# Recurrent stage of a two-block model: 32 by 32 triangles inverted by substitution on VectorE, one matrix a partition, instead of by products on TensorE

## The reference, cut to what matters

```python
for d in range(2):                       # forward, then reversed in time
    r, k, v = mix(p_r, ...), mix(p_k, ...), mix(p_v, ...)
    decay = jnp.exp(-jnp.exp(w_log)); a = jax.nn.sigmoid(...)
    kk = kk / jnp.maximum(jnp.sqrt(jnp.sum(kk * kk)), 1e-12)
    y_sum += wkv7_scan(rh, decay, kh, vh, -kk, kk * ah, reverse=(d == 1))

def step(state, inp):                    # of wkv7_scan, one token
    sa = jnp.einsum('bhvk,bhk->bhv', state, a_t)
    state = state * w_t + sa[..., None] * b_t + v_t[..., None] * k_t
    return state, jnp.einsum('bhvk,bhk->bhv', state, r_t)
```

## Time and profile before

| | before |
|---|---|
| median of 3 runs | 2783.99 us (2780.99 to 2785.55) |
| the profiled execution, its own time | 2784.29 us |
| its span | 2782.4 us |
| PE busy in the span | 2543.8 us (91%) |
| DVE busy | 1214.9 us (44%) |
| ACT busy | 771.4 us (28%) |
| POOL busy | 61.2 us (2%) |
| stage `rwkv7`: first instruction to first of the next stage | 1346.6 to 1650.9 us |

### The profile page before, as it was taken

How to read it: one execution, slowest core, us unless ns; L and a number is a source line. 1 busy time by engine, 2 the same in 40 slices (tenths; PEclk the granted TensorE clock), 3 DMA queues, 4 the chain that set the end, 5 groups by cost and what they waited for, 6 DMA issues and landing times. The chain is left out here.

```text
span 2782.4 us, 48899 instructions
## 1 busy us (share of the span) xinstructions
PE 2543.8 (91%) x21256; PEld 1789.0 (64%) x21256; DVE 1214.9 (44%) x2020; ACT 771.4 (28%) x1266; POOL 61.2 (2%) x52
## 2 busy tenths in 40 slices
PE   8998888899999999899899989979898998889888
PEld 7997677799999998677677757643333333333222
DVE  7764766544466652566544458531111111111113
ACT  4221354442343431355233236321000000000001
POOL 1000022100000000000000000010000000000000
PEclk9999899999999999999999989999999999999999
DMA  5445441355322223333212112489999999999997
GB/s 161 141 130 119 95 169 58 123 190 166 118 92 92 92 93 124 137 117 125 90 55 97 51 73 90 172 335 432 429 431 431 430 430 432 429 431 431 430 431 295
DMA packets 143797, 609.68 MB, mean 219 GB/s; under 512 B 37536, under 2 KB 59168, under 8 KB 118560
## 3 DMA queue, kind: packets, MB, share of 16 engines
q1 hardware_dynamic: 114672, 571.68, 52.8%
q10 hardware_dynamic: 28912, 34.88, 3.9%
HBM read 566.68 MB, written 37.47 MB: 217 GB/s over the span
## 5 line engine op out<-in xcount | busy, mean ns | idle before, releaser
L3838 PE MATMUL moe_bank<-moe_ring,xg 128*64 128x512 f32 x2048 | 492.2, 624 | 86.5 <-DMA moe_ring<-in_w_exp_up 85.6
L3838 PEld LDWEIGHTS moe_bank<-moe_ring,xg 128*64 128x64 f32 x2048 | 155.0, 142 | 365.9 <-issue 357.2
L4128 DVE TENSOR_TENSOR moe_sg<-moe_sg,moe_bank 64x512 f32<-64x512 f32 x64 | 44.1, 689 | 576.5 <-ACT moe_sg L3996 576.5
L3868 PE MATMUL moe_bank<-moe_ring,moe_act_t 128*64 128x512 f32 x1008 | 227.0, 592 | 0.0
L68 PE MATMUL ffn_prod<-ffn_x_low,ffn_w_high 128*128 128x258 f32 x704 | 200.1, 284 | 5.8 <-PEq L138 5.8
L69 PE MATMUL ffn_prod<-ffn_x_high,ffn_w_low 128*128 128x258 f32 x704 | 200.0, 284 | 0.0
L68 PE MATMUL in_bank<-x_low,in_w_high 128*128 128x264 f32 x640 | 184.8, 289 | 16.4 <-DVE in_w_low L987 9.2
L70 PE MATMUL ffn_prod<-ffn_x_high,ffn_w_high 128*128 128x258 f32 x704 | 199.2, 283 | 0.0
L70 PE MATMUL in_bank<-x_high,in_w_high 128*128 128x264 f32 x640 | 183.1, 286 | 0.0
L69 PE MATMUL in_bank<-x_high,in_w_low 128*128 128x264 f32 x640 | 182.6, 285 | 0.0
L4003 ACT COPY moe_act_t<-moe_bank 128x256 f32<-128x256 f32 x64 | 23.8, 372 | 508.6 <-PE moe_bank L3852 508.6
(11 more groups left out here) (592 smaller groups left out, 5293.5 us busy)
## 6 DMA issues: line engine op xcount, KB each, us to landing
moe_ring<-in_w_exp_gate SPq DMA_DIRECT2D x64, 2048.0 KB, 27.7
moe_ring<-in_w_exp_up SPq DMA_DIRECT2D x64, 2048.0 KB, 21.3
moe_ring<-in_w_exp_down SPq DMA_DIRECT2D x63, 2048.0 KB, 25.9
ffn_w<-in_w_up SPq DMA_DIRECT2D x44, 512.0 KB, 4.3
in_w<-in_w_in SPq DMA_DIRECT2D x40, 512.0 KB, 4.0
front_w<-in_w_in SPq DMA_DIRECT2D x32, 512.0 KB, 3.4
ffn_w<-in_w_down SPq DMA_DIRECT2D x16, 704.0 KB, 4.0
rw_w<-in_w_in SPq DMA_DIRECT2D x18, 512.0 KB, 4.0
```

What stands on the lines that cost most here:

```text
L3838: last = nc.tensor.matmul(bank[64 * g:64 * g + 64, s], xe[:, (e // BATCH) % 2, k, at:at + CAPACITY], ring[:, slot_of(n, g), k * HALF:(k + ...
L3868: last = nc.tensor.matmul(bank[64 * h:64 * h + 64, 3 + e % 2], act_t[:, s, j], weights[:, at:at + HALF], start=(c == 0 and j == 0), stop=( ...
L4128: nc.vector.tensor_tensor(sg[0:CAPACITY, s], sg[0:CAPACITY, s], bank[64:64 + CAPACITY, s], ALU.mult).then_inc(act_ready, 1)
```

## The change: what it does

- TensorE makes all triangles of a direction at once, ahead of everything (`lowers`), VectorE masks them into `lower` (`mask_lower`).
- SyncE stores them to DRAM (`tri`), in pieces of 32 floats, and loads them back as `flat`, one matrix of 1024 floats in each of 96 partitions.
- VectorE inverts the 96 matrices in place by substitution (`invert`): the diagonal is set to one, and for k = 1 to 30 a multiply of an outer-product shape and an add, k times (31 - k) elements each. The 60 instructions depend on one another and stand in three parts (22, 16, 22).
- SyncE stores the result and loads it back into `lower`, where `solve` reads it.
- The chain of products, its powers and sums, and their buffers are gone. `scores` no longer makes the triangles or their transposes.
- The 144 steps of side work are laid out anew: 40 ahead of the groups (`FIRST_STEPS`, five slots of one tile each), 10 in each group (4, 1, 4, 1) instead of 15 (1, 2, 2, 1, 1, 2, 1, 2, 1, 2), and 24 behind as before. The memory's tiles are the 13th to the 16th instead of the 5th to the 8th. `finish_ends` and `finish_rows` of a group now stand in the same group.
- ScalarE loads the table set that has both logarithm and exponential once, at the start of the stage.

```diff
-SIDE_FIRST = 4
+SIDE_FIRST = 12
-GROUP_STEPS = (1, 2, 2, 1, 1, 2, 1, 2, 1, 2)
+FIRST_STEPS = (8, 8, 8, 8, 8)
+GROUP_STEPS = (4, 1, 4, 1)
+SWEEPS = (range(1, 12), range(12, 20), range(20, RCHUNK - 1))
@@ sync
+                sp.dma_start(masks[:], masks_dram).then_inc(masks_loaded, 16)
+                load_w(0)
+                sp.dma_start(eye_head[:], eyes_dram).then_inc(masks_loaded, 16)
+                load_w(1)
+                store_lower(0)
+                store_lower(1)
+                load_flat(0)
+                for n in range(2, SIDE_TILES):
+                    load_w(n)
+                    if n == 5:
+                        store_flat(0)
+                        load_inverse(0)
+                        load_flat(1)
...
+                    if n == 11:
+                        store_flat(1)
+                        load_inverse(1)
@@ tensor
+                for d in range(2):
+                    lowers(d)
                 for x in range(RW_X):
                     turn(0, x)
                 scores(0)
                 starts(0)
+                for slot in range(len(FIRST_STEPS)):
+                    side(slot)
                 for g in range(G):
+                    slot = group_slot(g)
                     if g + 1 < G:
                         turn(g + 1, 0)
                         turn(g + 1, 1)
+                    solve(g)
                     if g + 1 < G:
                         turn(g + 1, 2)
                         scores(g + 1)
+                    side(slot)
                     if g + 1 < G:
                         starts(g + 1)
+                    side(slot + 1)
+                    finish_ends(g)
+                    side(slot + 2)
+                    finish_rows(g)
+                    side(slot + 3)
@@ vector
+                def invert(d, part):
...
+                    for k in SWEEPS[part]:
...
+                        dve.wait_ge(swept, made)
+                        nc.vector.tensor_tensor(terms, flat[0:MATRICES, upto, k].unsqueeze(2).broadcast_to(grid),
+                                                flat[0:MATRICES, k, beyond].unsqueeze(1).broadcast_to(grid), ALU.mult).then_inc(swept, 1)
+                        dve.wait_ge(swept, made + 1)
+                        nc.vector.tensor_tensor(flat[0:MATRICES, upto, beyond], flat[0:MATRICES, upto, beyond], terms,
+                                                ALU.add).then_inc(swept, 1)
...
+                for slot in range(len(FIRST_STEPS)):
+                    side(slot)
+                    if slot < len(SWEEPS):
+                        invert(0, slot)
                 for g in range(G):
+                    if 1 <= g <= len(SWEEPS):
+                        invert(1, g - 1)
                     if g + 1 < G:
                         mask(g + 1)
```

More of the change, by code:

```diff
@@ L2861, in _, with load_w @@
             def _(sp):
-                for n in range(SIDE_TILES):
+                def load_w(n):
                     if n >= 2:
@@ L3294, in first_inverse, with mask_lower @@
-                def first_inverse(g):
-                    dve.wait_ge(masked, 6 * (g + 1))
-                    nc.vector.tensor_tensor(ch[:, 1, :, P_PLACE], ch[:, 0, :, AT_ONE], eye_chunk.unsqueeze(1).broadcast_to(
-                        [P, heads_all, RCHUNK]), ALU.add).then_inc(inverse_ready, 1)
+                def mask_lower(d):
+                    dve.wait_ge(lower_made, d + 1)
+                    n = RW_X * (T // P)
+                    for e in range(2):
+                        nc.vector.tensor_tensor(lower[:, d, e], bank[:, LOWER_BANK[d] + e, 0:n * RCHUNK].rearrange(
+                            "p (n t) -> p n t", t=RCHUNK), masks[:, d, 1].unsqueeze(1).broadcast_to([P, n, RCHUNK]),
+                            ALU.mult).then_inc(lower_masked, 1)
@@ new lines, in invert @@
+                def invert(d, part):
+                    made = SWEPT * d
+                    if part == 0:
+                        dve.wait_ge(flat_loaded, 16 * (d + 1))
+                        nc.vector.memset(of_matrix[:, 0::RCHUNK + 1], 1.0).then_inc(swept, 1)
+                    made += 1 + 2 * sum(len(SWEEPS[n]) for n in range(part))
+                    for k in SWEEPS[part]:
+                        upto, beyond = slice(0, k), slice(k + 1, RCHUNK)
+                        if d == 1:
+                            k = RCHUNK - 1 - k
+                            upto, beyond = slice(k + 1, RCHUNK), slice(0, k)
+                        grid = [MATRICES, upto.stop - upto.start, beyond.stop - beyond.start]
+                        terms = sweep[0:MATRICES, 0:grid[1] * grid[2]].rearrange("p (r t) -> p r t", t=grid[2])
+                        dve.wait_ge(swept, made)
[4 more added lines that the diff above has]
+                                                ALU.add).then_inc(swept, 1)
+                        made += 2
@@ L4416, in laid_out @@
     d["ident"] = np.eye(P, dtype=f32)
-    d["rw_eyes"] = np.concatenate([np.tile(np.eye(n, dtype=f32), (P // n, 1)) for n in (HEAD_DIM, RCHUNK)] + [
-        np.repeat((n // RCHUNK % 2 == side).astype(f32)[:, None], RCHUNK, 1) for side in range(2)] + [
-        np.ones((P, RCHUNK), f32)], 1)
+    d["rw_eyes"] = np.tile(np.eye(HEAD_DIM, dtype=f32), (P // HEAD_DIM, 1))
     d["slots"] = np.broadcast_to(np.arange(1, CAPACITY + 1, dtype=f32), (P, CAPACITY))
```

311 lines of the change are left out of this document (126 added, 185 removed).

## The result

| | median (lowest to highest) | ratio to before (95% interval) |
|---|---|---|
| before, same chip, 4 runs | 2784.30 us (2780.99 to 2785.55) | |
| after, 4 runs | 2717.69 us (2715.53 to 2718.81) | 0.9762 (0.9745 to 0.9779) |
| after, its profiled execution | 2715.53 us, span 2713.7 | |

The change takes 66.6 us off, 2.4%. I had said 2721, in a range of 2705 to 2740.

A forecast was written before the change was run, and what follows sets the result against it. PE was taken to bound groups and scan, a chain of transfers and VectorE the opening. The stage would end at 1400.4 + 164.3 + 23.2 = 1587.9 against 1650.9, so 2784.3 - 63.0 gives 2721 us, range 2705 to 2740.

The forecast's parts named there:

- What bounds the kernel: Whole kernel: stages follow one another and PE bounds groups and scan, so time won there reaches the end.
- The groups and the scan: Eight groups and scan: less PE work, waits and low clock bring 270.2 us down to 164.3.
- the 2.0 for a low clock: Start of the groups: 4 us more at half clock behind the fifth tile cost 2.0 us.
- the wait of 1.5 in group 1: Group 1: VectorE's second-direction substitution delays the mask that starts needs, adding 1.5 us.
- other idle time: Groups: of 12.9 us idle, only the rounds' waits of 5.8 go; none of the rest is taken away.
- The opening: Before the groups: a chain through transfers and VectorE bounds, so the groups open at 1400.4.
- The step that failed: Opening: the fourth tile can start at 1379.9, and only the fifth waits, 3.5 us.
- the term for the clock: Fifth tile: half clock for 15 us after its wait, so the tile takes 11.2 us.
- The clock's rivals: Opening and group 1: no fall at the fifth tile, 2713.5 us, chance 0.13; two more falls, 2736, chance 0.12.
- The tail: Stage's end: the table load ahead of the exponentials goes, 1.3 us less, from 24.5 to 23.2.
- The third rival: Opening's stores: transfers in small pieces take 19 us each, total 2771 us, halfway 2745; chance 0.07.
- Slow instructions: Substitution: each instruction costs 0.1 us more than a plain one, total 2731 us; chance 0.09.

The follow-up runs named there:

- kernel 12: The changed kernel run again unchanged, on another chip: 2723.13 us, 0.9771 of the kernel before.
- kernel 3: The changed kernel with the second direction's substitution cut from 60 instructions to 6: 2718.24 us, 0.9742 of the kernel before.
- kernel 1: The kernel before with only the single table load for logarithm and exponential at the stage's start: 2785.24 us, one run.
- kernel 4: The changed kernel with the first direction's load waiting only for its own store and issued ahead of the second store: 2723.69 us, 0.9759 of before.
- kernel 6: The changed kernel with the triangles stored in pieces of 3072 bytes instead of 128: 2720.13 us, 0.9763 of the kernel before.
- kernel 5: The changed kernel with the first direction's substitution in five parts instead of three: 2721.20 us, 0.9769 of the kernel before.
- kernel 8: The changed kernel with the memory's splits and sums moved earlier, into groups 2 and 3: 2720.04 us, 0.9762 of the kernel before.
- kernel 9: The changed kernel with five substitution parts, the memory's work moved, six tiles ahead of the groups and 9 steps a group: 2728.11 us, 0.9787 of before.
- kernel 10: On top of kernel 9, the first direction's opening work put first, with four substitution parts: 2724.36 us, 0.9777 of the kernel before.
- kernel 11: On top of kernel 10, second triangles in halves, their substitution behind reading the ends, memory's work in group 3, steps 3, 1, 4, 1: 2715.88 us, 0.9743 of before.
- kernel 7: The changed kernel loading only a quarter of the weights for the third and later side-work tiles: 2715.92 us, one run.

## Why the prediction was right, point by point

- **What bounds the kernel.** Right. The stage got 67.0 us shorter and the execution 68.8, and TensorE's busy time in all fell by 68.4 (2543.8 to 2475.4): nothing behind the stage gave the gain back. The first weights of the expert layer were asked for 68.6 us earlier (1750.41 against the earlier trace rows).
- **The groups and the scan**: 164.3 said, 163.7 measured. Groups 0 and 2, with little idle time, took 16.0 and 16.2 us, as said. Inside the sum errors cancel: of the 2.0 for a low clock nothing came at 1400, but the clock stood at half for 3.4 us behind the wait for the rows in group 4, which costs at most 1.7 (in kernel 12 it did not fall there); of the wait of 1.5 in group 1 0.3 to 0.6 showed, and some 1.6 in the groups as a whole (kernel 3); that other idle time would stay at 7 us was too little, it is 10.1.
- **The opening**: 53.8 us said from the start of the stage to the groups, 52.4 measured. The steps erred one against the other. Stores landed 1.7 us late (1360.8): the second triangles waited for TensorE's two gaps, 4.9 us in all, and a store took 4.1, not 3.6. The substitution began 2.2 late, and its parts were right to 0.2 us each. The step that failed is that the fourth tile could start in time: it waited 2.6. Most of it is that the second part ended 1.9 late; the rest is that I let a tile wait for the split alone, while the wait ends with the reading of a tile (L3266), 0.6 behind the split. And the term for the clock was mis-sized: I took 15 us at half from the earlier trace rows; it was some 3, which gives back 3.9 in the fifth tile and the 2.0 behind it. The inverse was back at 1396.6 and not at 1393.9 (its store and load took 3.0 and 4.1), still 2.9 ahead of solve.
- **The clock's rivals.** Neither came as written. The clock fell at the fifth tile, but for 3 us, and once more, in group 4, for 3.4. So the opening came out 1.4 us shorter than said because the clock made good for the wait that I had missed: that is luck.
- **The tail**: 1.3 said, 3.3 measured to the next stage's start. The table load is worth 1.4 (kernels 1 and 4), and the rest is the clock of the variance products, which comes or not: another piece of luck, of 1.7. By the Trainium skill, "ScalarE: Activation LUTs", section "What ACT_TABLE_LOAD costs", the switch would be 2.66 us; kernel 4 against before shows 1.4.
- **Small pieces.** The third rival's price was 19 us a transfer; measured 4.1, and 2.6 in large pieces (kernel 6). The Trainium skill, "DMA: Bandwidth & Descriptors", section "Specifications", was right that pieces under 512 bytes cost; here it was 1.5 us a store, beneath other work. That they are read, modified and written no run shows.
- **Slow instructions.** None. 120 multiplies and adds took 0.36 us each from start to start; by my formula, with 165 elements on average, 0.37.
- **Sum**: 1587.9 said for the stage's end, 1583.4 measured: 1.9 from the opening, 0.6 from groups and scan, 2.0 from the tail. Another 1.2 came behind the stage, in the profiled execution.

## What to carry to other kernels

To invert on an engine with half its time free, and to lay out the side work anew, was worth 67 us, because what went stood on the engine that bounds. Not all of it is the substitution's: 1.4 us are the table load, and TensorE was busy at half clock for some 33 us of the stage before and 12 after, which is some 11 us by estimate, 1.7 of it in the tail. What the new layout alone would win in the kernel before was not run. Of some 43 us of its own the substitution shows 8 in the opening and, by the estimate of kernel 3, 1.6 in the groups. When you mend the waits that such a change leaves, ask of each what is late right behind it: here four of six mends (kernels 4, 5, 8, 9) removed or shortened a wait that the profile named and gained nothing, since another limit stood within 3 us or the work of an in-order engine only moved. Put long work of such an engine ahead of an instruction that waits for others, not behind it: that was a wait of 3.7 us in kernels 9 and 10, and gone in 11 (with three other edits).

## What the runs showed of the hardware

- **TensorE's instructions come in packets.** The profile's queues have one that carries them:

```profile
q8 instruction: 155, 2.54, 0.4%
```

  That is 16.4 KB a packet, and 19528 matmuls in 155 packets are 126 each (21256 in 169 before: 1728 more matmuls, 14 more packets). That it is TensorE's queue is inferred from these counts. The Trainium skill, "Runtime: NRT & Kernel Launch", section "Terms", says that instruction memory is refilled in blocks of 16 KiB; the trace agrees. Read in windows of 0.5 us, the packets of this stage up to 1500 are never closer than 3.4 us, in before, after and kernel 11. In after they stand in the windows from 1347.0, 1351.5, 1355.5 and 1359.5, and the gaps in the triangles end at 1349.88 and 1354.17. The gap in group 3 ends at 1460.97, behind a packet in the window from 1458.5, which came 6.6 us after the one before it. The other profiles bear this out. In the stage, the 14 of them have 98 waits for no work of 0.5 us or more; 96 end 2.1 to 3.0 us behind the start of such a packet, where only a seventh of the stage's time lies, and the two others are the waits of solve for the inverse in kernels 5 and 9. So small matmuls in a row, 384 records in 4.5 us of work, can outrun their own instructions. Why some packets come late, as in that gap, is open; the bytes of the weights are not the cause (kernel 7).
- **The clock's fall after a wait varies.** Behind 2.38 us it stayed at half for 14 us before, but for 7 in kernel 1, at the same place and behind the same wait:

```profile
1398.40:1412.20 13.80, 13.80 (x209) 11.07 (x204) 1.37 (x3) 3.43 (x8) 0.00 (x0) 0.51 0.01 2
...
1399.25:1406.15 6.90, 6.90 (x150) 5.77 (x150) 1.20 (x3) 1.52 (x4) 0.00 (x0) 0.51 0.08 30
1406.15:1412.00 5.85, 5.85 (x94) 4.90 (x93) 0.71 (x2) 1.82 (x5) 0.00 (x0) 1.00 0.01 3
```

  Behind 3.16 it stayed at half for 3 in after; behind 8.65 for 4.5 in kernel 5; behind 2.57 in after it didn't fall; behind 2.11 in group 4 it fell for 3.4 in after and not in kernel 12; behind 1.8 in the tail it fell in 6 profiles of 14, at 1.7 us each time. So a price taken from one such fall, as I took it from the earlier trace rows, is a guess.
